# Where the split activations lie in SBUF: both 16 KiB buffers moved to addresses 320 bytes past the weights modulo 512

## The chip, the cores and the metric

The kernel runs on one core of a Trainium2 chip. The metric is the device time of one execution in microseconds: median 1664.53 of three runs (1662.9 to 1668.57). The profile was taken in a further execution that took 1666.71 us, of which its span from the first to the last instruction is 1664.9 us.

## The reference, cut to what matters

Six blocks of a small transformer on 256 tokens with 1024 channels, all in float32: multi-head latent attention and a squared-ReLU MLP, an mLSTM mixer and a squared-ReLU MLP, then (second model part) gated MLP, short convolution, gated MLP, and gated MLP, sparse attention with three branches, gated MLP. Nearly all the arithmetic is a product of the activations with a weight matrix that is read once:

```python
def swiglu_ffn(x, w_in, w_out):
    gate, up = jnp.split(x @ w_in, 2, axis=-1)
    return (jax.nn.silu(gate) * up) @ w_out

def sqrelu_mlp(h, w1, w2):
    return jnp.square(jax.nn.relu(h @ w1)) @ w2
```

The softmax, the mLSTM recurrence and the compressed, selected and windowed branches of the sparse attention work on heads of 64 to 256 columns and are a small part of the time.

## The kernel before, in words

**Precision.** TensorE's float32r type takes a number in one pass but keeps fewer of its bits. So each operand is split in two: `hi` is the value rounded to float32r, `lo` is the rest. A product is `w_hi*x_hi + w_hi*x_lo + w_lo*x_hi`: three matmuls for each block of 128 x 128 weights and 256 tokens. The residual stream `x` lies in SBUF as eight chunks of 128 channels by 256 tokens. Its normed and split form lies in `xs`, chunk after chunk, 256 columns of `hi` and then 256 of `lo`. The outputs of the three attention-like mixers are split into `os` (also the input of the third gated MLP, whose source is `os_`), the hidden activations of the MLPs into `hs`.

**Weights.** 522 tiles of 128 x 1024 float32 (eight blocks of 128 columns) stream from HBM in the order of use through a ring of four slots: SyncE's queue loads `raw`, ScalarE writes `w_hi` (L510), VectorE subtracts for `w_lo` (L968; L448 on GpSimd for 46 tiles). TensorE waits for `lo_ready` of a tile, works through its eight blocks and signals `tile_done`; that frees the slots of `w_hi` and `w_lo`.

**TensorE's three ways of working.** `narrow_product` (L1651 to L1653) has the weights stationary and 256 columns of `xs` or `os` moving, three matmuls to a block; `feature` and `residual_one` call it. `product` (L1643, L1644) has `w_hi` stationary with `hi` and `lo` of `hs` together as 512 moving columns, then `w_lo` with the 256 of `hi`; `residual` calls it for the second layers of the MLPs. `token_major` (L1779 to L1781) has 128 tokens of `xs` or `os` stationary and 512 columns of weights moving. Each matmul has a load of its own stationary operand (a LDWEIGHTS, engine PEld in the profile), which runs while the matmul before it streams. The order on every engine is the order of the code; there is no planner.

**Where things lie.** Buffers get SBUF addresses (bytes from the start of a partition) in the order in which the program names them; a name in a `with ... pass` block gives its place back at once, so that the next one lies on top of it: `bias` on `os`, `xs` on `w1c_all`, `arena` on `hs`. Worked out from the sizes, with the base of 16512 for `raw0`:

| buffer | bytes | address before | modulo 512 | address after | modulo 512 |
|---|---|---|---|---|---|
| `raw`, 4 slots | 4 x 4096 | 16512 | 128 | same | 128 |
| `w_hi`, 4 slots | 4 x 4096 | 32896 | 128 | same | 128 |
| `w_lo`, 4 slots | 4 x 4096 | 49280 | 128 | same | 128 |
| `x` | 8192 | 65664 | 128 | same | 128 |
| `half`, `fsum`, `sq`, `sil` | 14 x 1024 | 73856 | 128 | 106944 | 448 |
| `con` | 6168 | 90400 | 288 | 123488 | 96 |
| `kT`, `vtok` | 2 x 4096 | 103840 | 416 | 136928 | 224 |
| `os`, `bias` | 16384 | 113312 | 160 | 90560 | 448 |
| `xs`, `w1c_all` | 16384 | 129696 | 160 | 74176 | 448 |
| `hs`, `arena` | 65536 | 146080 | 160 | 146592 | 160 |

Chunks of `xs`, `os` and `hs` are 2048 bytes apart and `lo` lies 1024 behind `hi`; blocks of weights are 512 bytes apart. So within these buffers the address modulo 512 is one and the same for every matmul: before, every moving operand from `xs`, `os` or `hs` begins 32 bytes past its weights modulo 512. The limits of 64 and 128 KiB are 65536 and 131072: before, `os` lies wholly between them and `xs` but for its first 1376 bytes beyond them.

```python
pe.matmul(out, w_hi[s][:, c:c + P], x_hi, start=first, stop=False)   # L1651: stationary, then moving
pe.matmul(out, w_hi[s][:, c:c + P], x_lo, start=False, stop=False)   # L1652
return pe.matmul(out, w_lo[s][:, c:c + P], x_hi, start=False, stop=last)   # L1653
```

Of the kernel before, what the change touches and what calls it, by code (L numbers as in the profile page):

```python
# [24 lines left out]
F32 = mybir.dt.float32  # L25
F32R = mybir.dt.float32r
# [4 lines left out]
P = 128  # L31
S = 256
TB = S // P
D = 1024
KD = D // P
# [8 lines left out]
H, NOPE, ROPE, VD = 16, 64, 32, 64  # L44
# [92 lines left out]
def build(nc, x_in, tiles, vecs, rows, consts, rel_bias, w1c_k, w1c_v, w2c_k, w2c_v, y_out):  # L137
    ctx = ExitStack()
    with ctx:
        def sb(name, shape, dt=F32):  # L140
            return ctx.enter_context(nc.sbuf_tensor(name, shape, dt))
# [7 lines left out]
        w_lo = [sb(f"w_lo{s}", [P, TILE], F32R) for s in range(RING)]  # L149
        x = sb("x", [P, KD * S])  # L150

        half = [sb(f"half{s}", [P, S]) for s in range(4)]
        fsum = [sb(f"fsum{s}", [P, S]) for s in range(4)]
        sq = [sb(f"sq{s}", [P, S]) for s in range(4)]
# [17 lines left out]
        kcT = sb("kcT", [P, G * NC])  # L172
        vc = sb("vc", [G * NC, G * DH])

        with nc.sbuf_tensor("os", [P, KD * 2 * S], F32R) as os_:
            pass
        bias = sb("bias", [P, H * S])
        with nc.sbuf_tensor("w1c_all", [P, 2 * 16 * P], F32) as w1c_all:
            pass
        xs = sb("xs", [P, KD * 2 * S], F32R)  # L180
        with nc.sbuf_tensor("hs", [P, FF1 * 2 * S], F32R) as hs:
            pass
        arena = sb("arena", [P, FF1 * 2 * S])
# [2025 lines left out]
```

## Time and profile before

| | |
|---|---|
| median of three runs | 1664.53 us |
| the profiled execution | 1666.71 us, span 1664.9 us |
| TensorE, matmuls | 1602.7 us busy (96% of the span), 11652 of them |
| TensorE, weight loads | 1510.1 us (91%) |
| VectorE | 1099.6 us (66%) |
| ScalarE | 885.4 us (53%) |
| GpSimd | 163.7 us (10%) |
| DMA | 282.81 MB, mean 170 GB/s |
| granted TensorE clock | 0.985 on the mean |

The duration that the profile gives to one matmul (some 281 ns for 256 columns) is from its issue to its last result, and the next one begins long before that end. What counts is the spacing from one matmul's start to the next one's. It is read from the number of matmuls in a stretch in which TensorE never rests, or from the starts in the timeline.

### The profile page before, as it was taken

The numbers are of one execution on the slowest core, as the hardware profiler recorded it, in microseconds if no ns is written. First come the engines' busy times: TensorE is split into PE (matmuls) and PEld (weight loads), VectorE is DVE, ScalarE is ACT, GpSimd is POOL, SyncE is SP. The second block draws the span as 40 slices with busy tenths as digits, with TensorE's granted clock in tenths as the row PEclk, the third lists the DMA queues.
The fourth block names the chain that finished last, engine by engine and source line by source line (L and its number), as shares of the span: only waits on it lengthen the run. The fifth ranks groups of instructions, "written<-read, shape, count | busy, mean of one in ns | idle before, by whom it ended". The sixth has DMA issues, their size and how long they took to land.

```text
span 1664.9 us, 33598 instructions
## 1 busy us (share of the span) xinstructions
PE 1602.7 (96%) x11652; PEld 1510.1 (91%) x11652; DVE 1099.6 (66%) x1770; ACT 885.4 (53%) x1468; POOL 163.7 (10%) x141
## 2 busy tenths in 40 slices
PE   7899999999999999999999999997999988799999
PEld 7789998977999899998999999897999867799997
DVE  6667766544876667667877666785566728676665
ACT  5676554535655445455446445544545546664443
POOL 1640000266000000000000000000000053300000
PEclk9999999989999999999999999998999989999999
DMA  6136566544566556556655555656455680055564
GB/s 228 64 82 199 188 190 190 176 131 135 178 190 188 191 176 198 182 187 203 191 188 189 190 188 187 206 182 196 145 189 186 210 171 15 1 175 186 184 197 142
DMA packets 81246, 282.81 MB, mean 170 GB/s; under 512 B 8848, under 2 KB 12432, under 8 KB 81168
## 3 DMA queue, kind: packets, MB, share of 16 engines
q1 hardware_dynamic: 77376, 276.88, 52.4%
q10 hardware_dynamic: 3792, 4.85, 1.7%
q8 instruction: 54, 0.88, 0.2%
q14 instruction: 24, 0.20, 0.0%
HBM read 280.12 MB, written 1.57 MB: 169 GB/s over the span
## 4 chain that ended last, share of the span: by engine, by line
PE 88%; DVE 5%; ACT 3%; issue 2%; DMA 1%; ACTq 1%; POOL 0%; DVEq 0%; SPq 0%; POOLq 0%
PE psum L1651 17%; PE psum L1653 17%; PE psum L1652 17%; PE psum L1643 17%; PE psum L1644 9%; PE psum L1779 2%; PE psum L1780 2%; PE psum L1781 2%; ACT arena L853 1%; DMA raw<-tiles 1%; DVE w_lo L968 1%; PE psum L2034 1%; PE psum L1941 1%; DVE arena L1517 0%; DVE arena L1516 0%
## 5 line engine op out<-in xcount | busy, mean ns | idle before, releaser
L510 ACT ACTIVATE w_hi<-raw 128x1024 fp32r<-128x1024 f32 x522 | 550.5, 1056 | 462.8 <-PE psum L1653 266.3
L968 DVE TENSOR_TENSOR w_lo<-raw,w_hi 128x1024 fp32r<-128x1024 f32 x476 | 582.0, 1223 | 229.0 <-ACT w_hi L510 228.2
L1651 PE MATMUL psum<-xs,w_hi 128*128 128x256 f32 x1960 | 550.7, 281 | 6.1 <-DVE w_lo L968 5.0
L1653 PE MATMUL psum<-xs,w_lo 128*128 128x256 f32 x1960 | 549.8, 280 | 0.0
L1652 PE MATMUL psum<-xs,w_hi 128*128 128x256 f32 x1960 | 547.9, 280 | 0.0
L1643 PE MATMUL psum<-hs,w_hi 128*128 128x512 f32 x1216 | 421.9, 390 | 0.0
L1651 PEld LDWEIGHTS psum<-xs,w_hi 128*128 128x128 f32 x1960 | 369.6, 189 | 7.2 <-DVE w_lo L968 5.5
L1652 PEld LDWEIGHTS psum<-xs,w_hi 128*128 128x128 f32 x1960 | 369.7, 189 | 0.2
L1653 PEld LDWEIGHTS psum<-xs,w_lo 128*128 128x128 f32 x1960 | 369.2, 188 | 0.0
L1644 PE MATMUL psum<-hs,w_lo 128*128 128x256 f32 x1216 | 343.4, 282 | 0.0
L1643 PEld LDWEIGHTS psum<-hs,w_hi 128*128 128x128 f32 x1216 | 228.3, 188 | 47.1
L448 POOL TENSOR_TENSOR w_lo<-raw,w_hi 128x1024 fp32r<-128x1024 f32 x46 | 110.3, 2411 | 1228.1 <-ACT w_hi L510 1198.0
L1644 PEld LDWEIGHTS psum<-hs,w_lo 128*128 128x128 f32 x1216 | 230.5, 190 | 0.0
L1651 PE MATMUL psum<-os,w_hi 128*128 128x256 f32 x544 | 154.5, 284 | 1.6 <-DVE os L1158 1.6
L1652 PE MATMUL psum<-os,w_hi 128*128 128x256 f32 x544 | 152.7, 281 | 0.0
L1653 PE MATMUL psum<-os,w_lo 128*128 128x256 f32 x544 | 152.6, 281 | 0.0
L1651 PEld LDWEIGHTS psum<-os,w_hi 128*128 128x128 f32 x544 | 103.2, 190 | 2.5 <-DVE os L1158 2.4
L1652 PEld LDWEIGHTS psum<-os,w_hi 128*128 128x128 f32 x544 | 103.2, 190 | 0.0
L1653 PEld LDWEIGHTS psum<-os,w_lo 128*128 128x128 f32 x544 | 103.1, 189 | 0.0
L991 DVE SCALAR_TENSOR_TENSOR xs<-x,vec,xs 128x256 fp32r<-128x256 f32 (+1 forms) x80 | 38.1, 482 | 51.7 <-ACT xs L524 51.7
L524 ACT ACTIVATE xs<-x,vec (+1 forms) x80 | 40.2, 509 | 54.3 <-DVE x L1058 31.2
L1106 DVE TENSOR_TENSOR fsum<-psum,sil 128x256 f32<-128x256 f32 x88 | 37.4, 425 | 46.0 <-PE psum L1653 44.7
(282 smaller groups left out, 1643.8 us busy)
## 6 DMA issues: line engine op xcount, KB each, us to landing
raw<-tiles SPq DMA_DIRECT2D x522, 512.0 KB, 4.2
bias<-bias_dram ACTq DMA_DIRECT2D x8, 256.0 KB, 12.5
x<-x_in SPq DMA_DIRECT2D x4, 256.0 KB, 5.7
y_out<-x SPq DMA_DIRECT2D x8, 128.0 KB, 3.5
con<-consts SPq DMA_DIRECT2D x1, 771.0 KB, 9.2
bias_dram<-bias_row ACTq DMA_DIRECT2D x1, 512.0 KB, 7.2
row<-rows SPq DMA_DIRECT2D x1, 192.0 KB, 9.2
vec<-vecs SPq DMA_DIRECT2D x1, 80.5 KB, 1.9
```

The lines of the kernel that those rows point to most:

```text
L448: pool.tensor_tensor(w_lo[s][:, :], raw[s][:, :], w_hi[s][:, :].bitcast(F32), ALU.subtract).then_inc(lo_ready, 1)
L510: act.activation(w_hi[s][:, :], raw[s][:, :], ACT.Copy).then_inc(hi_ready, 1)
L524: act.activation(dst, src, ACT.Copy, scale=gain).then_inc(xhi_ready, 1)
L968: dve.tensor_tensor(w_lo[s][:, :], raw[s][:, :], hi_of(w_hi[s][:, :]), ALU.subtract).then_inc(lo_ready, 1)
L991: dve.scalar_tensor_tensor(out=dst, in0=src, scalar=gain, in1=hi_of(hi), op0=ALU.mult, op1=ALU.subtract).then_inc(xs_ready, 1)
L1106: dve.tensor_tensor(f, bank(b, 0, S), sil[u // 2][:, :] if u % 2 else rb[:, :], ALU.mult).then_inc(out_read, 1)
L1643: pe.matmul(bank(out_bank), w_hi[s][:, c:c + P], src[:, chunk:chunk + 2 * S], start=first, stop=False)
L1644: return pe.matmul(bank(out_bank, 0, S), w_lo[s][:, c:c + P], src[:, chunk:chunk + S], start=False, stop=last)
L1651: pe.matmul(out, w_hi[s][:, c:c + P], x_hi, start=first, stop=False)
L1652: pe.matmul(out, w_hi[s][:, c:c + P], x_lo, start=False, stop=False)
L1653: return pe.matmul(out, w_lo[s][:, c:c + P], x_hi, start=False, stop=last)
L1779: pe.matmul(out, x_hi, w_hi[s][:, col:col + 512], start=c == 0, stop=False)
```

## The change

It moves names in the list of buffers and adds two unused ones as padding: `apart_x` of 320 bytes ahead of `xs` and `apart_h` of 192 bytes ahead of `hs`. `xs` and `os` come ahead of the small buffers and now both lie between 64 and 128 KiB, 320 bytes past the weights modulo 512 (448 against 128). The small buffers follow and so have other addresses too. `hs` and `arena` lie 512 bytes further on, so that their address modulo 512 is what it was.

```diff
         x = sb("x", [P, KD * S])
 
+        sb("apart_x", [P, 80])
+        with nc.sbuf_tensor("w1c_all", [P, 2 * 16 * P], F32) as w1c_all:
+            pass
+        xs = sb("xs", [P, KD * 2 * S], F32R)
+        with nc.sbuf_tensor("os", [P, KD * 2 * S], F32R) as os_:
+            pass
+        bias = sb("bias", [P, H * S])
         half = [sb(f"half{s}", [P, S]) for s in range(4)]
...
         kcT = sb("kcT", [P, G * NC])
         vc = sb("vc", [G * NC, G * DH])
 
-        with nc.sbuf_tensor("os", [P, KD * 2 * S], F32R) as os_:
-            pass
-        bias = sb("bias", [P, H * S])
-        with nc.sbuf_tensor("w1c_all", [P, 2 * 16 * P], F32) as w1c_all:
-            pass
-        xs = sb("xs", [P, KD * 2 * S], F32R)
+        sb("apart_h", [P, 48])
         with nc.sbuf_tensor("hs", [P, FF1 * 2 * S], F32R) as hs:
             pass
         arena = sb("arena", [P, FF1 * 2 * S])
```

No instruction is added, removed or moved on any engine, no wait changes, and no shape: the rows of all five engines read the same before and after but for the line numbers, which are two higher.

## Rows read from the trace of the kernel before

**Rows 1.** The page: busy time by engine; the chain that ended last.

```profile
PE 1602.7 (96%) x11652; PEld 1510.1 (91%) x11652; DVE 1099.6 (66%) x1770; ACT 885.4 (53%) x1468; POOL 163.7 (10%) x141
...
PE 88%; DVE 5%; ACT 3%; issue 2%; DMA 1%; ACTq 1%; POOL 0%; DVEq 0%; SPq 0%; POOLq 0%
```

**Rows 2.** TensorE's groups: line, shapes, xcount | busy us, mean ns | idle before.

```profile
L1651 PE MATMUL psum<-xs,w_hi 128*128 128x256 f32 x1960 | 550.7, 281 | 6.1 <-DVE w_lo L968 5.0 <-DVE xs L991 1.1
...
L1643 PE MATMUL psum<-hs,w_hi 128*128 128x512 f32 x1216 | 421.9, 390 | 0.0
...
L1651 PE MATMUL psum<-os,w_hi 128*128 128x256 f32 x544 | 154.5, 284 | 1.6 <-DVE os L1158 1.6
...
L1779 PE MATMUL psum<-w_hi,xs 128*128 128x512 f32 x128 | 55.3, 432 | 0.2 <-DVE w_lo L968 0.2
...
L1779 PE MATMUL psum<-w_hi,os 128*128 128x512 f32 x34 | 14.3, 419 | 2.3 <-issue 2.3
```

**Rows 3.** Windows, TensorE alone: stretches of `narrow_product` without a pause.

```profile
core 0: us, PE busy (x), PEclk, DMA share, GB/s
140.00:220.00 80.00, 80.00 (x688) 1.00 0.61 188
446.00:526.00 80.00, 80.00 (x689) 1.00 0.65 194
626.00:736.00 110.00, 110.00 (x936) 1.00 0.62 192
900.00:1010.00 110.00, 110.00 (x946) 1.00 0.58 190
1185.00:1265.00 80.00, 80.00 (x688) 1.00 0.58 189
1486.00:1596.00 110.00, 110.00 (x945) 1.00 0.61 193
...
872.00:890.00 18.00, 18.00 (x155) 1.00 0.52 160
```

**Rows 4.** Timeline at 180 us, TensorE: start us, duration us, line, operands.

```profile
180.01 0.28 PE L1651 MATMUL psum<-xs,w_hi 128*128 128x256 f32 x1
180.12 0.28 PE L1652 MATMUL psum<-xs,w_hi 128*128 128x256 f32 x1
180.25 0.28 PE L1653 MATMUL psum<-xs,w_lo 128*128 128x256 f32 x1
180.36 0.28 PE L1651 MATMUL psum<-xs,w_hi 128*128 128x256 f32 x1
```

**Rows 5.** Timeline at 300 us, TensorE in `residual`: two starts five blocks apart.

```profile
299.68 0.39 PE L1643 MATMUL psum<-hs,w_hi 128*128 128x512 f32 x1
299.91 0.28 PE L1644 MATMUL psum<-hs,w_lo 128*128 128x256 f32 x1
...
301.41 0.39 PE L1643 MATMUL psum<-hs,w_hi 128*128 128x512 f32 x1
```

**Rows 6.** Timeline at 60 us, TensorE in `token_major`: two starts eight matmuls apart.

```profile
59.62 0.40 PE L1781 MATMUL psum<-w_hi,os 128*128 128x512 f32 x1
...
61.49 0.40 PE L1780 MATMUL psum<-w_lo,os 128*128 128x512 f32 x1
```

**Rows 7.** Transposes and attention values, float32: runs in the timeline, then groups.

```profile
1391.12 0.82 PE L2019 MATMUL psum<-con,arena 128*128 128x128 f32 x6
...
L2019 PE MATMUL psum<-con,arena 128*128 128x128 f32 x96 | 13.1, 273 | 0.0
```

**Rows 8.** Window of the first gated MLP, all engines; then the two splitting groups.

```profile
640.00:680.00 40.00, 40.00 (x342) 40.00 (x342) 25.89 (x36) 19.13 (x28) 0.00 (x0) 1.00 0.61 189
...
L968 DVE TENSOR_TENSOR w_lo<-raw,w_hi 128x1024 fp32r<-128x1024 f32 x476 | 582.0, 1223 | 229.0 <-ACT w_hi L510 228.2
...
L510 ACT ACTIVATE w_hi<-raw 128x1024 fp32r<-128x1024 f32 x522 | 550.5, 1056 | 462.8 <-PE psum L1653 266.3 <-PE psum L1644 113.0 <-PE psum L1781 54.7
```

## The prediction

> **What bounds the kernel now.** I read the page first. TensorE is busy 96% of the span, and the chain that ended last is 88% TensorE, against 5% for VectorE and 3% for ScalarE [rows 1]. Then the groups by form: the matmuls of `xs` and `os` wait for others 6.1 and 1.6 us in all at their first line [rows 2], so in the long products nobody feeds TensorE too slowly. The windows say the same: in six stretches of 80 to 110 us it is busy all the time at the full granted clock, the 2.4 GHz level [rows 3]. What counts is the time from one matmul's start to the next, its spacing. In the window of the first gated MLP VectorE is busy 25.89 of 40 us and ScalarE 19.13, and their splitting of a weight tile takes 1.22 and 1.06 us [rows 8], while TensorE works at a tile for 24 spacings, 2.8 us. DMA is at 0.61. All have room: if the spacing shrinks by a tenth, none of them becomes the bound.
>
> **The spacings before.** A window also counts the two or so matmuls that were in flight when it opened (0.28 us of duration at 0.117 us of spacing is 2.4). The six windows of [rows 3] hold 4892, less 14, in 570 us: 116.9 ns. It isn't one value: 936 less 2.4 in 110 us is 117.8 ns, 688 less 2.4 in 80 us is 116.7. The timeline shows the second kind beating unevenly, starts 0.11, 0.13 and 0.11 us apart [rows 4] (it rounds to 0.01). The 512-column matmul of `residual` and its 256-column partner take 1.73 us for five pairs, 346 ns a pair [rows 5], of which the first is 0.23. In `token_major`, eight matmuls of 512 columns take 1.87 us, 234 ns each [rows 6]. In a run of six float32 transposes, each with a weight load of 128 columns like all the others, the starts lie (0.82 less one duration of 0.273) / 5 = 109 ns apart [rows 7]. So TensorE can start a load and a matmul every 109 ns, and the float32r products with 256 moving columns need 8 ns more.
>
> **The change part by part.**
>
> *No work changes.* No instruction, wait, shape or queue is touched. Only where reads and writes land differs. The terms are those in which TensorE reads `xs` or `os`.
>
> *Three-matmul products.* 1960 blocks on `xs` and 544 on `os` [rows 2], three matmuls each: 7512 at 116.9 ns, 878 us, more than half the span. What the new place does to the spacing no row of before shows, since there all these reads stand at one distance from their weights, 32 bytes modulo 512. Bounds: at best the spacing falls to the 109 ns of the transposes, 7512 x 7.9 = 59 us less. At worst each weight load gets the excess that it has in `token_major`: 234 against some 229 to 230 ns for the same 512 columns in `residual` (346 less one 256-column spacing of 116.9). There the moving operand lies 32 bytes before the stationary one, not behind. That is 4 to 5 ns for each matmul, 7512 x 5 = 38 us more. Between the two I take 114 ns, the length of the short beat of the uneven pattern (0.11 us, [rows 4]). The argument for a gain at all is that pattern. The same code on the same buffers settles at 116.7 in one stage and at 117.8 in another, with the other engines no busier, and it beats unevenly inside. That looks like the load's reads and the moving reads getting in each other's way, sometimes in one step and sometimes in another, and a fixed shift of 288 bytes between the two streams is what would change this. Why it should change for the better I can't show; only that the excess of 8 ns leaves more room below than the spread of the rows leaves above. Term: 7512 x 2.9 = 21.8 us less.
>
> *Token-major products.* 128 groups on `xs` and 34 on `os` [rows 2], three matmuls each: 486 at 234 ns. They go from 480 (that is, 32 before) to 192 bytes modulo 512. I take the figure of `residual`, 229: 486 x 5 = 2.4 us less; bounds from 8 us less (the excess over twice 109 gone) to 2.4 more.
>
> *`residual`'s products on `hs`* keep their distance: 1216 pairs, nothing. Bounds: 1 us either way.
>
> *The 64 to 128 KiB limits by themselves.* `os` lies there already, `xs` doesn't. The third gated MLP reads `os`: 688 matmuls in 80 us at 1185, just as `xs` in 140 to 220 [rows 3]. So at a distance of 32 this costs and gives nothing.
>
> *The small buffers, `con`, `kT`, `vtok`, `bias`.* VectorE and ScalarE read them elsewhere. They have room in the long stages [rows 8], which hides it; where they bound (between stages, 8% of the chain, some 130 us) no row ties a duration to an address. I count nothing, 1 us either way.
>
> A rule speaks against any effect. The trace has shown ScalarE and VectorE busy and idle beside an unchanged full TensorE [rows 3, 8]. The Trainium skill (SBUF — State Buffer, Who interferes with whom) gives TensorE two independent read ports, one for the moving operand and one for weight loads, and says that "PE and ACT never wait on anyone". By that the address is indifferent and the sum would be zero; this is the rival of no effect below.
>
> The floor of 109 ns is read from [rows 7]. The Trainium skill (TensorE: Matmul & The Clock Gate, Back-to-back issue gap) puts the gap of a lone matmul at N/2.4 + 2.5 ns; for 256 columns this is 109.2, which the transposes' 109 would fit and the 116.9 of float32r does not. By it the best case is the same 58 us.
>
> Sum: 1666.7 (the profiled execution) - 21.8 - 2.4 = 1642.5. The median of the runs lies 2.2 below the profiled execution, so 1640 is the forecast.
>
> **Rivals.**
>
> *No effect.* The distance modulo 512 doesn't matter. For it: the equal pace of `os` and `xs`, though they lie 16 KiB apart and on two sides of 128 KiB, and the evenness of the windows whatever slot the weights are in. Also the one stage that runs `narrow_product` on `hs` (872 to 890 us: 155 less 2.4 in 18 us, 118 ns) is like the slower of the `xs` stages [rows 3]. The 8 ns would be the price of float32r itself. Against it: two paces from identical code. Time: 1664, within 5.
>
> *Slower by the same mechanism.* The new distance makes the two read streams of TensorE meet more often. Place: every matmul of `xs` and `os`. Price: 7.5 us for each ns of spacing; it decides as soon as the spacing in the windows is over 117.6 ns. If all stages fall into the slower known pattern, 117.8, it is 7512 x 0.9 = 7 us, 1671; with the full excess of `token_major`, 38 us, 1703; in the middle, 2.5 ns, 19 us, 1683. For it: `token_major` shows that some arrangement costs more than this one. Against: it differs in more than distance (which operand is the long one), so its excess may not be one of address at all.
>
> *The excess goes away altogether.* 109 ns as for the transposes: 59 and 8 us less, 1598. For it: transposes read `con`, which lies between 64 and 128 KiB, against stationary operands at many distances, and run at 109. Against: they move half the columns, so their reads leave gaps that 256 float32r columns don't.
>
> **How the numbers follow.** A difference under 0.3%, 5 us, is what a measurement of this kernel can't tell from none. A gain in part, like the forecast: 0.38. The excess all gone or nearly: 0.08. No effect: 0.29. Slower: 0.25, of which a third by under 10 us. Faster by over 0.3% is then 0.46 less what the partial gain leaves within 5 us, and no effect takes that up: 0.45, 0.30, 0.25. The time is the likeliest case's, 1640, whose own range is 1615 to 1658. For 8 in 10 the range must take in no effect and the milder slow cases at one end and most of the full gain at the other: 1602 to 1682.
>
> **What would show it right or wrong.** Right: windows of 80 us in stages on `xs` and `os` hold 704 matmuls instead of 688, `residual` still 346 ns a pair, `token_major` near 229 ns, everything between the stages as before. No effect: 688 again. Slower: under 684. Wrong in mechanism though not in sign: if `hs` changes its pace as well, whose distance is kept, or if the time comes from VectorE's or ScalarE's durations. A gain of over 30 us would mean that the 8 ns were mostly collisions.

## The result and the profile after

The kernel after takes 1670.13 us (median of 11 runs, 1668.28 to 1673.66), the kernel before 1665.93 (11 runs, 1662.9 to 1668.57): a ratio of 1.0029, 95% interval 1.002 to 1.0039. It is slightly slower. The profiled execution has a span of 1669.1 us, 4.2 more than the 1664.9 of before.

The page of the kernel after, its busy line and the shares of the chain:

```profile
PE 1610.7 (97%) x11652; PEld 1516.9 (91%) x11652; DVE 1100.8 (66%) x1770; ACT 885.8 (53%) x1468; POOL 163.9 (10%) x141
...
PE 89%; DVE 5%; ACT 3%; issue 1%; DMA 1%; POOL 0%; DVEq 0%; ACTq 0%; SPq 0%
```

Beside [rows 1] the number of instructions is the same on every engine, VectorE and ScalarE are busy within 1.2 us of before, and TensorE is busy 8 us more. The chain keeps its shares.

The stages go by short names from here on. `up_0` and `up_1` are the first layers of the squared-ReLU MLPs, `glu_0` to `glu_3` those of the gated MLPs. `wo_a`, `wo_m` and `wo_n` are the output projections of the three mixers, `dkv` and `mqk` input projections of the first and the second, `cin` and `cout` the two projections of the convolution.

Windows of TensorE alone in the kernel after, over the stretches of [rows 3] (window, busy us, count, granted clock, DMA share, GB/s), and one of `wo_m` at 424 us:

```profile
140.00:220.00 80.00, 80.00 (x680) 1.00 0.61 190
446.00:526.00 80.00, 80.00 (x681) 1.00 0.60 190
626.00:736.00 110.00, 110.00 (x937) 1.00 0.61 188
900.00:1010.00 110.00, 110.00 (x935) 1.00 0.58 188
1185.00:1265.00 80.00, 80.00 (x681) 1.00 0.58 185
1486.00:1596.00 110.00, 110.00 (x936) 1.00 0.57 186
872.00:890.00 18.00, 18.00 (x157) 1.00 0.48 157
...
424.00:440.00 16.00, 16.00 (x144) 1.00 0.62 194
```

Five of the six long windows lost 7 to 11 matmuls; the one at 626, which had been the slow one with 936, has 937. All six now agree with 117.8 ns to within two matmuls of the count. The short window at 872 us is `cout`, whose operand `hs` kept its distance of 32 bytes: it has 157 instead of 155, and over the whole stage 116.7 ns instead of 117.8. And 144 matmuls in 16 us are 113 ns, a pace that [rows 3] nowhere has.

Starts of TensorE in `residual` can be read as a window too (pairs of 512 and 256 columns), and in `token_major` from two starts eight matmuls apart, both in the kernel after:

```profile
230.00:310.00 80.00, 80.00 (x463) 1.00 0.61 190
```

```profile
63.68 0.39 PE L1783 MATMUL psum<-w_hi,os 128*128 128x512 f32 x1
...
65.55 0.39 PE L1782 MATMUL psum<-w_lo,os 128*128 128x512 f32 x1
```

463 less 2.4, halved, are 230 pairs in 80 us: 347 ns, as in [rows 5]. Eight matmuls in 1.87 us are 234 ns, to the hundredth the same as in [rows 6].

I then took the mean spacing of each kind over the whole trace. For `narrow_product` it is 116.98 ns before and 117.61 after, without the stops: in each of the two traces some 50 to 60 spacings longer than 0.17 us are left out. Times its 7704 matmuls (the 7512 on `xs` and `os` and `cout`'s 192 on `hs`) that gives 901.2 us before and 906.0 after, 4.8 more; I call this the sum. The pairs of `residual` took 421.5 and 421.4. So the spacing of the three-matmul products accounts for the 4.2 us of the span; everything else together, stops included, comes to some half a microsecond less.

### The profile page after: what moved, and what is told of

Read it like the earlier page. It is cut to its first block, busy times and chain, and to the rows that moved or that the text cites. A ratio compares the mean times of both kernels' runs of the same rounds, so it can differ in the third digit from the quotient of the medians.

```text
span 1669.1 us, 33598 instructions
## 1 busy us (share of the span) xinstructions
PE 1610.7 (97%) x11652; PEld 1516.9 (91%) x11652; DVE 1100.8 (66%) x1770; ACT 885.8 (53%) x1468; POOL 163.9 (10%) x141
## 4 chain that ended last, share of the span: by engine, by line
PE 89%; DVE 5%; ACT 3%; issue 1%; DMA 1%; POOL 0%; DVEq 0%; ACTq 0%; SPq 0%
PE psum L1654 18%; PE psum L1653 18%; PE psum L1655 17%; PE psum L1645 16%; PE psum L1646 9%; PE psum L1781 2%; PE psum L1782 2%; PE psum L1783 2%; ACT arena L855 1%; DMA raw<-tiles 1%; DVE w_lo L970 1%; PE psum L2036 1%; PE psum L1943 1%; DVE arena L1519 0%; DVE arena L1518 0%
```

## The experiments

Every spacing below is read as above: the mean time from one start to the next in a stage, without stops, from one profiled execution. The sum over the 7704 is given where it decides.

**The same kernels once more.** Nothing is edited.

> The kernel before, unchanged, for a second look at its spacings. In its first profile the first MLP's up-projection (140 to 220 us) held 688 matmuls in 80 us (116.7 ns apart) and the first gated MLP (626 to 736 us) 936 in 110 us (117.8 ns). If each kernel's pace is fixed by where its buffers lie, the same stages show the same two values again, within one matmul. If TensorE settles by chance at each start of a stage into one of a few rhythms, some stages change from 116.7 to 117.8 or back.

> The changed kernel, unchanged, for a second look. In its first profile all long stages on xs and os ran at 117.8 ns a matmul but for the second projection of attention-like outputs (414 to 441 us), which ran at 113.9. If the rhythm is fixed by the addresses and the program, the same stages show the same values; if it is chance, the 113.9 turns up in other stages or not at all.

Before took 1664.47 us (one run, span 1662.7), after 1672.21 (span 1670.4). Windows of before again, then of after again:

```profile
626.00:736.00 110.00, 110.00 (x945) 1.00 0.57 191
```

```profile
22.00:28.00 6.00, 6.00 (x55) 1.00 0.53 172
424.00:440.00 16.00, 16.00 (x138) 1.00 0.60 198
```

The first gated MLP of before, 936 matmuls in one execution, has 945 in the other: the same instructions on the same addresses ran at 117.7 ns once and 116.7 once. So did `mqk`, `cin` and `cout`. In the kernel after `wo_m` lost its fast pace (138 instead of 144) and the short `dkv` at 22 us found it (55 in 6 us). The pace of a stage isn't fixed by the program; the address fixes which paces there are to choose from, as the sweeps below show. `cout` tells the same: it runs at 117.8 ns in one execution of before and at 116.7 in the other, so its change in the kernel after needs no cause in the edit. The sums are steadier than the stages: 901.2 and 899.0 before, 906.0 and 906.5 after. The spans follow them: the second executions lie 7.7 us apart, their sums 7.5.

**Place without distance, distance without place.** The first kernel has the buffers in the order of after, but `xs`, `os` and the small buffers 288 bytes lower, so that the distance is 32 again. The second is the kernel before with gaps that only make the distance 320. "Distance" is always how far the activations lie past the weights, and the weights never move in any of these kernels.

```diff
 e3, against the kernel after
-        sb("apart_x", [P, 80])
+        sb("apart_x", [P, 8])
...
-        sb("apart_h", [P, 48])
+        sb("apart_h", [P, 120])
 e4, against the kernel before
+        sb("apart_x", [P, 72])
         with nc.sbuf_tensor("os", [P, KD * 2 * S], F32R) as os_:
...
+        sb("apart_h", [P, 56])
         with nc.sbuf_tensor("hs", [P, FF1 * 2 * S], F32R) as hs:
```

> xs and os between 64 and 128 KiB as in the changed kernel, but at the old distance of 32 bytes past the weights modulo 512. If the distance makes the difference: as the kernel before, ratio 1.000 within 0.1%, long stages mostly at 116.7 ns. If the place between 64 and 128 KiB (or the small buffers' new addresses) makes it: as the changed kernel, ratio 1.003, all at 117.8 ns.

> Old order of buffers, with padding so that os and xs lie 320 bytes past the weights modulo 512 (os still between 64 and 128 KiB, xs nearly all behind). If the distance makes the difference: as the changed kernel, ratio 1.003, long stages at 117.8 ns, perhaps one at 113.9. If the place makes it: ratio 1.000, mostly 116.7 ns.

Place only: 1665.89 us (12 runs), ratio to before 0.9996 (0.9985 to 1.0007). Distance only: 1672.46 (6 runs), ratio 1.0039 (1.0024 to 1.0054). Windows of TensorE, place only, then distance only:

```profile
446.00:526.00 80.00, 80.00 (x688) 1.00 0.58 197
626.00:736.00 110.00, 110.00 (x945) 1.00 0.58 196
900.00:1010.00 110.00, 110.00 (x946) 1.00 0.57 193
```

```profile
446.00:526.00 80.00, 80.00 (x681) 1.00 0.58 196
626.00:736.00 110.00, 110.00 (x937) 1.00 0.56 193
424.00:438.00 14.00, 14.00 (x126) 1.00 0.66 226
```

The first are the counts of before (the 945 is that of its second execution), the others those of after, `wo_m` at its 113 ns included. The 288 bytes are the whole effect; the 64 to 128 KiB and the small buffers' move by 32 KiB are none. One thing these two can't tell apart, nor can any kernel below: since the weights stay 128 bytes past a multiple of 512, a distance is also an address of the activations modulo 512. Whether the place relative to the weights counts, or the activations' own address, was not tested; it would take a kernel that moves the weights.

**Which distance gives which pace.** If distance decides, it can be chosen. Three sweeps give each stage a distance of its own, in steps of 32 bytes: the buffers become 512 bytes longer, and `DIST` names, by the stage that writes the operand, how far into the buffer it begins.

```diff
-        xs = sb("xs", [P, KD * 2 * S], F32R)
+        DIST = {'ffn_0': 0, 'mix_1': 64, 'ffn_1': 96, 'pre_0': 128, ...}
+        xs_all = sb("xs", [P, KD * 2 * S + P], F32R)
...
+        def X(name):
+            d = DIST[name] // 4
+            return xs_all[:, d:d + KD * 2 * S]
...
```

> Each stage reads its split activations at a distance of its own from the weights, modulo 512 (all between 64 and 128 KiB for xs and os): up_0 0, mqk 64, up_1 96, glu_0 128, cin 160, cout 128, glu_1 192, kvc 224, glu_2 256, glu_3 288, wo_a 448, wo_m 480, wo_n 416; the second layers on hs at 0, 64, 96, 160, 192, 224. If the distance sets which rhythms TensorE can fall into: long stages show values of their own between 109 and 122 ns a matmul, the same distance the same small set of values wherever it is used, and the stages of one distance differ from those at 32 (116.7 or 117.8) and 320 (117.8 or 113.3). If the distance only shifts the odds between the same few rhythms: nothing but 113.3, 116.7 and 117.8. The pair of matmuls on hs is 346.7 ns at 32; if its streams meet in the same way it varies too, else it is 346.7 everywhere.

> As the first sweep with other distances: up_0 352, mqk 384, up_1 416, glu_0 448, cin 480, cout 320, glu_1 320, kvc 0, glu_2 32, glu_3 224, wo_a 64, wo_m 96, wo_n 128; second layers on hs at 256, 288, 320, 352, 384, 416. Under the distance theory 320 shows 117.8 (or 113.3) in glu_1 and now also in cout, which read hs at 32 before and ran at 116.7; 32 shows 116.7 or 117.8 in glu_2; 0 in kvc and 224 in glu_3 show what up_0 and kvc show in the first sweep. If the rhythm belongs to the stage and not to the distance, each stage keeps the value that it has in the changed kernel.

> A third assignment: up_0 256, mqk 192, up_1 288, glu_0 64, cin 352, cout 192, glu_1 128, kvc 416, glu_2 96, glu_3 384, wo_a 0, wo_m 160, wo_n 320; second layers on hs at 448, 480, 32, 0, 128, 320. Nearly every distance of the first two sweeps now stands in another stage. Distance theory: same distance, same set of spacings. Stage theory: same stage, same spacing.

They took 1681.47, 1678.45 and 1685.63 us (one run each; most distances in them are bad ones). The map, in ns, each distance put together with the one 256 bytes on. In its last column too the distance is that of the activations past the weights, though there the activations are stationary; the prediction counts `token_major` the other way round, and its 480 and 192 are 32 and 320 here:

```text
distance mod 256   three-matmul spacing   pair on hs   token_major
  0                120.0                  353.3        227.4 to 227.7
 32                116.7 or 117.8         346.7        233.3
 64                113.3 or 117.8         353.3        233.3 to 233.5
 96                120.0                  350
128                118.7 (once 120.0)     351          232.3 to 232.6
160                118.7 (once 117.3)     346.7        233.4 to 233.6
192                113.3 or 117.8         353.3        229.3 to 229.7
224                118.3                  346.7 (at 480: 353.3)   233.3
```

Windows behind it. First sweep: distance 0, 192, 256; second: 448; third: 256 and 192.

```profile
150.00:220.00 70.00, 70.00 (x585) 1.00 0.57 190
912.00:1022.00 110.00, 110.00 (x936) 1.00 0.59 191
1190.00:1250.00 60.00, 60.00 (x503) 1.00 0.53 179
```

```profile
632.00:742.00 110.00, 110.00 (x973) 1.00 0.61 195
```

```profile
150.00:220.00 70.00, 70.00 (x586) 1.00 0.59 192
330.00:346.00 16.00, 16.00 (x144) 1.00 0.57 189
```

At 448 the gated MLP has 973 matmuls in 110 us against 936 to 946 before: 113.3 ns, and 585 in 70 us is 120.1 at 0. Distances 256 apart behave alike, but for the three exceptions in the table. The paces are steps: three matmuls take 340, 350, 353.3, 355, 356 or 360 ns, and two distances, 64 and 192, have the fastest and the 353.3 both.

In the first sweep, at 192, the second gated MLP changes its pace in front of our eyes. The timeline around the norm's sum (`ssq,ones`), a float32 matmul that adds up the squares of the activations near the stage's start:

```profile
906.23 0.28 PE L1666 MATMUL psum<-xs,w_hi 128*128 128x256 f32 x1
...
907.47 0.28 PE L1668 MATMUL psum<-xs,w_lo 128*128 128x256 f32 x1
907.59 0.59 PE L1684 MATMUL psum<-ssq,ones 128*128 128x256 f32 x2
...
908.14 0.28 PE L1667 MATMUL psum<-xs,w_hi 128*128 128x256 f32 x1
...
909.55 0.28 PE L1667 MATMUL psum<-xs,w_hi 128*128 128x256 f32 x1
```

Eleven spacings in 1.24 us are 112.7 ns before it, twelve in 1.41 us are 117.5 behind it, and so it stays to the stage's end (936 in the window above). So it is everywhere: the eleven profiles that aren't sweeps have 268 rows of 40 or more three-matmul starts without an interruption, and each keeps one pace from its tenth start to its end. At 32 that is 116.7 or 117.8 ns, at 320, 448 and 192 it is 113.3 or 117.8, and the odds differ: 7 of 72 rows took the fast one at 320, 69 of 118 at 448 and 192 (the kernels below).

**The fast pace everywhere?** The stages' distance set to 448, then to 192 (`residual`'s pairs stay at 32, `cq` at 256):

```diff
+        DIST = {'mix_0': 448, 'cq': 256, 'o_a': 448, 'ffn_0': 448, 'down_0': 32, ...}
 e6: 192 in place of each 448
```

> xs and os (and hs where the convolution's output projection reads it) all 448 bytes past the weights modulo 512; the second layers on hs stay at 32; the first mixer's token-major reads at 256. In the sweeps 448 gave 113.3 ns in three stages of three, 7704 three-matmul intervals against 116.9 before. If the distance sets the rhythm: 7704 x 3.5 = 27 us less than before, ratio 0.984. If TensorE falls back to 117.6 to 117.8 in most long stages, as it does at 320 and as one of four stages did at 192: ratio 1.000 to 1.004.

> The same with 192 instead of 448, that is 256 bytes further. In the sweeps every distance behaved like the one 256 bytes on (0 and 256: 120.0; 96 and 352: 120.0; 128 and 384: 118.7; 32 and 288: 116.7; 64 and 320: 117.8 or 113.3). If the period is 256: the same rhythms 113.3 and 117.8 as at 448, and the ratio lies between 0.984 and 1.004, according to how many stages catch the fast one. If the period is 512 a rhythm of its own appears.

At 448: 1655.25 us (12 runs, 1649.46 to 1666.62), ratio 0.9943 (0.9925 to 0.9961). At 192: 1654.01 (10 runs, 1644.64 to 1665.39), ratio 0.9939 (0.9915 to 0.9963). Windows at 448:

```profile
145.00:200.00 55.00, 55.00 (x488) 1.00 0.60 201
626.00:736.00 110.00, 110.00 (x937) 1.00 0.57 195
900.00:1010.00 110.00, 110.00 (x936) 1.00 0.58 194
1478.00:1586.00 108.00, 108.00 (x956) 1.00 0.59 199
```

The first and last run at 113.3 ns, the middle two at 117.8: about half of the work takes the fast pace. The sum is 890.7 us, 10.5 less than before, and the span 1653.7 is 11.2 less. No other engine stopped it: where the pace is 113.3 they keep up. `token_major` went from 233.3 to 229.3 ns (227.5 at `cq`'s 256), some 2 us over its 486 matmuls, but from its starts to the next ones, waits and all, it took 141.4 us against 141.8.

**Finer steps, and the pairs.** Steps of 4 bytes around 448 and around 32:

```diff
+        DIST = {..., 'ffn_0': 464, 'down_0': 48, 'pre_0': 456, 'out_1': 28, 'post_0': 448, 'mix_0': 452, ...}
 s5: 'ffn_0': 28, 'down_0': 284, 'ffn_1': 68, 'pre_0': 36, 'post_0': 4, ...
```

> A finer sweep, xs and os at 464, 432, 440, 456, 472, 444, 448, 424, 448, 460, 444, 436, 428, 468 (in the order up_0, mqk, up_1, glu_0, cin, cout, glu_1, kvc, glu_2, nq, glu_3, wo_a, wo_m, wo_n), second layers on hs at 48, 40, 36, 28, 24, 288. If what counts is a line or bank of 16 bytes or more, distances within one 16-byte step behave alike and 448 is one of several; if every 4 bytes count, the spacing changes from one to the next. 448 in glu_1 and glu_2 again: 113.3 if it is stable, else 117.8.

> A last sweep over distances between those tried: three-matmul stages at 28 (up_0), 60 (mqk), 68 (up_1), 36 (glu_0), 92 (cin), 124 (cout), 4 (glu_1), 156 (kvc), 220 (glu_2), 252 (glu_3), 12, 20, 100 (wo_a, wo_m, wo_n), pairs at 284, 20, 156, 220, 60, 12. Period of 256: 284 shows 343.4 ns a pair like 28. If only multiples of 64 have a fast rhythm, nothing here is under 116.7; if some distance has the fast one alone, its stage shows 113 or less from the start.

1687.86 and 1687.06 us. The three-matmul spacing is 120.0, 118.5, {113.3, 117.8}, 122.1, 120.0 ns at 440, 444, 448, 452, 456 bytes; 123.3, 117.7, 122.1, 117.1, 121.1 at 4, 12, 20, 28, 36. A single word moves it by several ns, and nothing beats 192 and 448. For the pairs 28, 60 and 284 bytes give 343.3 to 343.4 ns, against 346.7 at 32; but the pairs are as touchy: 24 and 36, four bytes below 28 and above 32, both give 360. A window of the fifth sweep, pairs at 284:

```profile
235.00:305.00 70.00, 70.00 (x410) 1.00 0.57 189
```

(410 less 2.4, halved, in 70 us is 343.5 ns.) So, as the kernel at 448, but with the pairs at 28:

```diff
-        'down_0': 32, 'down_1': 32, 'out_0': 32, 'out_1': 32, 'out_2': 32, 'out_3': 32
+        'down_0': 28, 'down_1': 28, 'out_0': 28, 'out_1': 28, 'out_2': 28, 'out_3': 28
```

> As e5_all_448, but the second layers read hs 28 bytes past the weights modulo 512 instead of 32. In the fine sweep one such stage (176 pairs) ran at 343.4 ns a pair against 346.7 at 32, 360 at 24 and 360 at 36. If this holds in all six, 1216 pairs x 3.3 ns = 4.1 us less than e5, ratio to the kernel before 0.992; if it was that one stage's luck, 0.994 as e5. xs and os again settle at 113.3 or 117.8 stage by stage, not in the same stages as in e5.

1649.09 us (5 runs, 1647.51 to 1652.75), ratio to before 0.991 (0.9895 to 0.9925): it is faster than both kernels. Its windows, a long stage at either pace and the pairs:

```profile
626.00:734.00 108.00, 108.00 (x955) 1.00 0.61 199
895.00:1005.00 110.00, 110.00 (x936) 1.00 0.57 192
230.00:310.00 80.00, 80.00 (x468) 1.00 0.57 188
```

The sum over the three-matmul products is 885.7 us (15.5 less than before), over the pairs 417.4 (4.1 less), together 19.6; the span is 19.3 less. All six `residual` stages keep 343.3 ns; no second pace showed.

**What chooses the pace?** In that kernel the first two weight tiles of a stage run side by side, and the norm's sum stands inside them, ahead of their last block. One kernel works through the first tile alone and puts the sum behind it, one makes the interruption longer:

```diff
 e8b, against the kernel with pairs at 28
-                paired = norm_ is not None and outs > 1 and name != "dq"
+                paired = False
 e9b, against the kernel with pairs at 28
-                        ins = pe.matmul(bank(RB, 0, S), ones[:, :], ssq[:, :], start=True, stop=True)
+                        for _ in range(3):
+                            ins = pe.matmul(bank(RB, 0, S), ones[:, :], ssq[:, :], start=True, stop=True)
```

> As e7 (448, pairs at 28), but the first two weight tiles of a stage aren't interleaved: the first tile is worked through alone and the sum for the norm comes behind it. If the choice of rhythm falls at the restart behind the sum: other stages run at 117.8 than in e7 (there up_0, up_1, glu_1, wo_n), perhaps all or none. If it falls elsewhere (by chance at the start of a stage): again about a third of the stages at 117.8. Time: a stage loses some 1 to 2 us of overlap at its start in eight stages, so with the same share of fast stages 1655 to 1665; with all fast ones 10 us less.

> As e7, but the sum for the norm is computed three times in a row into the same place, 9 stages x 2 more float32 matmuls (two passes each) of 0.43 us, 8 us more. If the restart behind the sum decides and depends on how the queue of weight loads stands after it: the stages behind it fall into one rhythm more evenly than in e7, all 113.3 (ratio to before 0.990) or all 117.8 (1.008). If not: as e7 with 8 us more, 0.996.

1661.32 us (10 runs), ratio 0.9985 (0.9969 to 1.0001), and 1648.62 (4 runs), ratio 0.9896 (0.9861 to 0.9931). Mean spacing by stage in ns, one execution each (`kr`, `dkv`, `cin`, `kvc`, `wo_n` and the gates are in the sum but not in the table):

```text
stage   before  again | after  again | 448    192    448,28 not paired  sum x3
wo_a    116.8   116.8 | 117.8  117.7 | 117.7  117.7  113.9    117.7     117.7
up_0    116.7   116.7 | 117.8  117.8 | 113.6  113.6  117.5    113.5     113.6
mqk     117.8   116.7 | 117.8  117.8 | 113.3  113.3  113.3    113.4     117.8
wo_m    116.8   116.7 | 113.9  117.8 | 113.6  117.4  113.6    117.4     113.6
up_1    116.7   116.7 | 117.5  117.8 | 117.5  113.6  117.5    113.5     113.4
glu_0   117.7   116.7 | 117.8  117.8 | 117.8  113.5  113.4    113.4     117.6
cout    117.8   116.7 | 116.7  116.7 | 113.3  113.3  113.3    117.8     113.3
glu_1   116.7   116.7 | 117.8  117.8 | 117.6  117.6  117.6    113.5     113.4
glu_2   116.7   116.7 | 117.6  117.6 | 114.4  116.9  113.6    116.4     116.8
glu_3   116.7   116.7 | 117.8  117.8 | 113.5  113.5  113.5    117.7     113.5
sum us  901.2   899.0 | 906.0  906.5 | 890.7  886.1  885.7    886.5     885.3
```

Both edits change which stages are fast. All three big stages that were slow (`up_0`, `up_1`, `glu_1`) become fast in both, and others turn slow instead, among them `cout` and `glu_3` in the one, `mqk` and `glu_0` in the other. The sums hardly differ. A value well between 113.3 and 117.8 is a mixture. In `glu_2`, which other work interrupts several times, the kernel at 192 has both paces, 113 ns and then 117.7:

```profile
1135.00:1146.00 11.00, 11.00 (x100) 1.00 0.62 207
...
1170.00:1250.00 80.00, 80.00 (x682) 1.00 0.56 187
```

So the pace isn't chosen once for a stage; it can change at each interruption. Since the same kernel also chooses differently from one execution to the next, one profile each can't tell the edit's hand from that; what steers the choice stays open. The kernel that isn't paired is slower for another reason: its span is 12.0 us longer at a sum only 0.8 larger, and TensorE waits more, 9.3 instead of 4.6 us at the first line on `xs` and 2.6 instead of 1.0 for `ssq`; from each start to the next, stops and all, its three-matmul products take 916.6 us instead of 904.0. Its norm's sum's row, then that of the tripled one. The profile has two records for each of these float32 matmuls, so 54 are 27 of them; they are busy 7.7 us longer than the single ones:

```profile
L1684 PE MATMUL psum<-ssq,ones 128*128 128x256 f32 x18 | 6.2, 429 | 2.6 <-DVE ssq L1083 2.6
```

```profile
L1685 PE MATMUL psum<-ssq,ones 128*128 128x256 f32 x54 | 13.4, 385 | 1.0 <-DVE ssq L1083 1.0
```

The 8 us more that I expected of the tripled sum did not come: the ratio was to be 0.996 and is 0.9896. The profiled execution has a span 4.6 us longer than that with the single sum at equal spacing, but the median of four runs, 1641 to 1652 us, is no longer than its 1649.09. Against the spread that the paces make, four runs can't settle what the extra sums cost.

## Why the prediction was wrong

*What bounds the kernel.* Right. Spacing of TensorE's matmuls is the term that moved, and nothing else: 4.8 us of spacing for 4.2 of span.

*No work changes; pairs on `hs`; place; small buffers.* Right, each at nothing. Counts and busy times of the other engines stand, the pairs differ by 0.1 us in 421, and place alone gives 0.9996. The sign that I had set for a wrong mechanism, a change of pace on `hs`, did show in `cout`, but the kernel before makes the same change from one execution to the next.

*The mechanism.* Right in that the address decides. Where the activations lie modulo 256, with the weights in place, sets the spacing, 113.3 to 123.3 ns with nothing else changed, and several paces come from identical code. That TensorE's two read streams get in each other's way was my reading of it and is not shown: no kernel moved the weights, and no view shows the reads. The Trainium skill (SBUF — State Buffer, Who interferes with whom) says that "PE and ACT never wait on anyone"; the traces agree as far as other engines go, for whole stages keep one pace while VectorE and ScalarE go busy and idle beside them (25.89 and 19.13 of 40 us in [rows 8]), but what I had made of it, that the address is then indifferent, they refute.

*The step that failed: "Between the two I take 114 ns".* The runs show 117.63 on average for the 7512 matmuls that the term counts, against 116.96 before: a term of +5.0 us in place of -21.8 (+4.8 with `cout`'s 192, which went the other way). The pace that I forecast exists at this distance (113.3 ns, in `wo_m` of one execution and `dkv` of another), but at 320 bytes the long stages took 117.8 nearly throughout in all three profiles, those of the kernel after twice and that of distance alone. My arguments were the uneven beat, and that an excess of 8 ns leaves more room below than above. Neither is a reason for a direction: the beat only said that something can vary. The sweeps show why: of the seven other distances modulo 256 in steps of 32, five cost more than either pace at 32 (but for one stage of 117.3 at 416), and the two that have 113.3 at all, 64 and 192, have 117.8 beside it. A shift without a reason lands more often on a worse distance than on a better one, as 32 was already among the better.

*"I take the figure of `residual`, 229", for `token_major`.* Wrong: 233.3 ns at both distances. The reading behind it was wrong as well. I had taken 346 less a three-matmul spacing as the price of 512 columns, but the two move apart: with the activations 192 past the weights the token-major products do take 229.3 to 229.7, and there the pairs take 353.3 instead of 346.7. Numbers of one product aren't parts of another's.

*The rivals.* The mild case of "slower by the same mechanism", all stages in the known slower pace, gave 1671, and 1670.13 was measured; its bound, slower from 117.6 ns, was just met. I had given it a third of 0.25. The case of no effect is excluded by the interval, though the ratio stays under the 0.3% that I had set as the least that one could tell. The excess never went away: the fastest three-matmul pace in any stage is 113.3 ns, 4 above the transposes' 109 of [rows 7]. That 109 was a doubtful floor besides, and the 109.2 that the prediction sets beside it is for 256 columns, while the transposes move 128. Where float32 moves 256 columns in the kernel before, two starts lie 0.60 - 0.39 = 0.21 us apart, twice as far:

```profile
1392.00 0.60 PE L2006 MATMUL psum<-kT,arena 128*128 128x256 f32 x2
```

So the 109 goes with 128 float32 columns, and no run shows what the least for 256 float32r columns is.

What the rows could have told: before already had 116.7 in most stages, close to its better pace, so a distance with the slower one everywhere could cost 7 us, and a gain needed a pace that no row had. That argues for the sign that came, or for a small number in either direction, not for the middle of a one-sided range.

## What to carry to other kernels

When TensorE is busy all the time, read its spacing by stage from the starts, not its busy time: steps such as 113.3, 116.7, 117.8 and 120.0 ns are paces of its own, and a change of addresses moves a kernel between them with no instruction changed. Sweep the address of the activations past the weights on the chip, a distance for each stage in one kernel, and set each kind of product to its own best (here 448 or 192 bytes for three matmuls, 28 for pairs, with the weights at 128 modulo 512). Don't argue the direction of such a change from the room on either side; and profile twice before a stage's pace is laid to an edit.

## What was unexpected of the hardware

The paces are exact: at a distance of 32, 64, 96, 192 or 0 bytes three matmuls take 340, 350, 353.3 or 360 ns, and TensorE holds one until something breaks the row. The map nearly repeats after 256 bytes (three exceptions), yet 4 bytes in it (448 to 452) are worth 113.3 to 122.1 ns. The same kernel at the same addresses takes different paces in different executions, stage by stage, and where both paces of a distance lie far apart the runs spread: 1649 to 1667 us at 448 and 1645 to 1665 at 192, against 1663 to 1670 for the kernel before beside them. What happens inside TensorE to make a step of 3.3 or 10 ns in three matmuls no view shows, and what decides at a restart was not settled. A kernel held at 113.3 in every stage would come out some 12 us below the 1649.09 (an estimate: 7704 x 1.6 ns, from the mean of 114.97 in that kernel); none of those run here did.
